# Norms of the keys by one value a token and head, a norm joined to the stage after it, a gate row folded into the experts' sum

## The reference, cut to what matters

```
# first_block, last line
return _rmsnorm(x, final_norm_w)
# second_block
hl = rms_norm(xl, norm1_gain) * (1.0 + sc1l) + sh1l        # 256 latents
hc = rms_norm(xc, norm1_gain) * (1.0 + sc1c) + sh1c        # 256 tokens of ctx
pl = hl @ w_in;  pc = hc @ w_in
# in the rwkv mixer: 512 tokens, 4 heads of 64
kk = hd(k * kk_scale)
kk = kk / jnp.maximum(jnp.sqrt(jnp.sum(kk * kk, axis=-1, keepdims=True)), 1e-12)
# the end
xl = xl + g2l * hierarchical_moe(h2l, *moe_w)
```

## Time and profile before

| | us |
|---|---|
| median of 3 runs | 2254.02 |
| lowest, highest | 2249.06, 2260.88 |
| profiled execution | 2261.8 |
| its span, from the first to the last instruction | 2260.0 |
| TensorE products / weight loads, busy | 2002.8 / 1682.6 |
| VectorE, ScalarE, GpSimd, busy | 1441.5, 1098.9, 146.7 |
| mean granted TensorE clock | 0.928 |

### The profile page before, as it was taken

The page is one execution under the profiler, slowest core; times in us unless marked ns, Lnnn a source line. Parts: engine busy times, 40 slices in busy tenths (PEclk is TensorE's granted clock), DMA queues, the critical chain, the costliest instruction groups (busy, mean ns, idle before and its releaser), DMA issues. The chain is left out here.

```text
span 2260.0 us, 36963 instructions
## 1 busy us (share of the span) xinstructions
PE 2002.8 (89%) x15254; PEld 1682.6 (74%) x15254; DVE 1441.5 (64%) x1794; ACT 1098.9 (49%) x1333; POOL 146.7 (6%) x151
## 2 busy tenths in 40 slices
PE   5788899899788899899959895798899999999997
PEld 5586677899677677799848664686778788788785
DVE  0264345787355444688447938764778788787886
ACT  0353343565254343466346433212567677676674
POOL 0000000000000000000004603620000000000000
PEclk8799799899899889999979987899899999999998
DMA  9764264545266237444342120000689899799896
GB/s 382 275 210 149 94 215 149 192 182 182 104 237 219 100 122 251 157 166 182 130 141 86 55 73 11 14 19 12 229 295 375 300 351 374 272 370 338 303 375 231
DMA packets 153800, 447.54 MB, mean 198 GB/s; under 512 B 10032, under 2 KB 12720, under 8 KB 151088
## 3 DMA queue, kind: packets, MB, share of 16 engines
q1 hardware_dynamic: 153648, 445.41, 54.9%
HBM read 444.33 MB, written 1.05 MB: 197 GB/s over the span
## 5 line engine op out<-in xcount | busy, mean ns | idle before, releaser
L212 DVE TENSOR_TENSOR me_wlow<-me_w,me_whigh 128x2048 fp32r<-128x2048 f32 (+1 forms) x203 | 451.9, 2247 | 107.7 <-ACT me_whigh L207 107.5
L207 ACT ACTIVATE me_whigh<-me_w 128x2048 fp32r<-128x2048 f32 (+1 forms) x203 | 380.2, 1885 | 133.5 <-PE ps L220 124.3
L218 PE MATMUL ps<-me_whigh,me_xhigh 128*128 128x512 f32 x512 | 206.9, 404 | 11.9 <-PEq L119 11.9
L218 PE MATMUL ps<-up_xhigh,ffn_whigh 128*128 128x256 f32 x704 | 201.8, 287 | 8.6 <-DVE ffn_wlow L212 7.0
L220 PE MATMUL ps<-me_whigh,me_xlow 128*128 128x512 f32 x528 | 208.6, 395 | 0.0
L219 PE MATMUL ps<-me_wlow,me_xhigh 128*128 128x512 f32 x512 | 202.0, 394 | 0.0
L219 PE MATMUL ps<-up_xlow,ffn_whigh 128*128 128x256 f32 x704 | 201.0, 286 | 0.0
L220 PE MATMUL ps<-up_xhigh,ffn_wlow 128*128 128x256 f32 x704 | 200.9, 285 | 0.0
L212 DVE TENSOR_TENSOR ffn_wlow<-ffn_w,ffn_whigh 128x2048 fp32r<-128x2048 f32 (+1 forms) x72 | 149.3, 2110 | 60.7 <-ACT ffn_whigh L207 60.6
L212 DVE TENSOR_TENSOR mix_wlow<-mix_w,mix_whigh 128x1024 fp32r<-128x1024 f32 (+2 forms) x116 | 140.4, 1214 | 70.7 <-ACT mix_whigh L207 70.5
L207 ACT ACTIVATE ffn_whigh<-ffn_w 128x2048 fp32r<-128x2048 f32 (+1 forms) x72 | 123.2, 1759 | 47.8 <-PE ps L220 47.8
(11 more groups left out here) (664 smaller groups left out, 4233.6 us busy)
## 6 DMA issues: line engine op xcount, KB each, us to landing
me_w<-w_exp_gate SPq DMA_DIRECT2D x34, 2048.0 KB, 9.6
me_w<-w_exp_up SPq DMA_DIRECT2D x34, 2048.0 KB, 10.2
me_w<-w_exp_down SPq DMA_DIRECT2D x32, 2048.0 KB, 10.2
mix_w<-w_mix SPq DMA_DIRECT2D x108, 512.0 KB, 4.2
mix_aside<-ada_w SPq DMA_DIRECT2D x96, 512.0 KB, 4.6
ffn_w<-ffn_w_up SPq DMA_DIRECT2D x20, 2048.0 KB, 7.6
ada_w<-ada_first SPq DMA_DIRECT2D x12, 2048.0 KB, 23.2
ffn_w<-ffn_w_down SPq DMA_DIRECT2D x8, 2048.0 KB, 7.8
```

The costliest lines, as they stand in the source:

```text
L207: return nc.scalar.activation(high, x, ACT.Copy)
L212: return nc.vector.tensor_tensor(low, x, high.bitcast(F32), ALU.subtract)
L218: nc.tensor.matmul(out, lh, rh, start=start, stop=False)
```

## The change

The last norm of the first block loses its own block and its code moves into `second_projections` (`final_act`, `final_dve`); the transfers are issued there in the order final, vectors, ctx, rows, consts, masks, weights, and each engine waits for the last four small ones at its planned place 13.0 (`arrived`), GpSimd at its start. The norms' planned times go from 1.0 and 2.5 to 4.6 and 7.9, the weights' clock from 17 to 19. The keys' sum of squares is taken with the squares as the stationary operand and `head_pick` (two columns) as the moving one, so that it comes out with tokens on partitions, one value a token and head, 16 a partition; Sqrt, bound and reciprocal work on those, VectorE spreads them over 64 columns each, TensorE transposes the result in eight tiles, and VectorE multiplies `kk` by it out of PSUM. In the experts, g_row is multiplied in when the sum is taken out of PSUM, the additions go straight to x, and each quarter of x is stored as its addition ends.

```diff
-def first_output(core, I, x, coming):
-                for dst, src in coming:
-                    sp.dma_start(dst, src).then_inc(here, 16)
-                sp.wait_ge(here, 16 * len(coming))
...
-        pieces.clock = 17.0
+        pieces.clock = 19.0
...
-                                 (2.5, 1.0)[s], ((0, 1, 2, 3), (4, 5, 6, 4))[s], started) for s in range(2)]
+                                 (7.9, 4.6)[s], ((0, 1, 2, 3), (4, 5, 6, 4))[s], started, (None, final_scaled)[s]) for s in range(2)]
...
+        def final_act(act):
+            yield 0.0
+            for t in range(TT):
+                nc.scalar.activation(hT[1][:, 4 * t:4 * t + 4, :].rearrange("p k n -> p (k n)"), x[:, t, :], ACT.Square,
+                                     accum_out=final_rs[:, t:t + 1]).then_inc(final_squared, 1)
+            yield 2.8
+            act.wait_ge(final_meaned, 1)
+            nc.scalar.activation(final_rs, final_rs, ACT.Sqrt).then_inc(final_rooted, 1)
+
+        def final_dve(dve):
+            yield 2.4
+            dve.wait_ge(final_squared, TT)
+            nc.vector.tensor_scalar(final_rs, final_rs, 1.0 / DM, EPS, ALU.mult, ALU.add).then_inc(final_meaned, 1)
+            yield 3.2
+            dve.wait_ge(final_rooted, 1)
+            nc.vector.reciprocal(final_rs, final_rs).then_inc(final_inverted, 1)
+            dve.wait_ge(final_inverted, 1)
+            dve.wait_ge(final_here, 16)
+            for t in range(TT):
+                nc.vector.scalar_tensor_tensor(out=x[:, t, :], in0=x[:, t, :], scalar=final_rs[:, t:t + 1], in1=final_row,
+                                               op0=ALU.mult, op1=ALU.mult).then_inc(final_scaled, 1)
+
+        def arrived(eng):
+            yield 13.0
+            eng.wait_ge(rest_here, 16 * 4)
+
         def context_act(act):
-            yield 2.4
+            yield 7.8
...
         def setup_dve(dve):
-            yield 0.0
+            yield 2.0
+            dve.wait_ge(vectors_here, 16)
...
+            yield t_low + 12.0
+            pe.wait_ge(kk_own, 4)
+            pe.wait_ge(gate_read, 1)
+            for c in range(NT4):
+                for hp in range(2):
+                    mm = nc.tensor.matmul(low_bank(0)[:, 4 * c + 2 * hp:4 * c + 2 * hp + 2], kn[:, hp, c * P:(c + 1) * P],
+                                          consts["head_pick"], start=True, stop=True)
+            mm.then_inc(kk_summed, 1)
             for hp in range(2):
-                yield t_low + 12.0 + 1.2 * hp
-                pe.wait_ge(kk_own, 4)
+                yield t_keys + 18.0 + 1.2 * hp
+                pe.wait_ge(key_own, spread_made)
                 pe.wait_ge(gate_read, hp + 1)
-                nc.tensor.matmul(low_bank(hp), consts["head_ones"], kn[:, hp], start=True, stop=True).then_inc(kk_summed, 1)
+                for c in range(NT4):
+                    mm = nc.tensor.transpose(low_bank(hp)[:, c * P:(c + 1) * P], kk_spread[:, c, hp], ident)
+                mm.then_inc(kk_summed, 1)
...
             yield t_keys + 16.0
-            dve.wait_ge(kk_rooted, 2)
-            mine(V.tensor_scalar(kn, kn, 1e-12, None, ALU.max))
+            dve.wait_ge(kk_rooted, 1)
+            mine(V.tensor_scalar(kk_rs, kk_rs, 1e-12, None, ALU.max))
             dve.wait_ge(key_own, own)
-            mine(V.reciprocal(kn, kn))
-            yield t_keys + 24.0
+            mine(V.reciprocal(kk_rs, kk_rs))
             dve.wait_ge(key_own, own)
-            mine(V.tensor_tensor(kk, kk, kn, ALU.mult))
+            mine(V.tensor_copy(kk_spread.rearrange("p c h (r n) -> p (c h r) n", r=2), kk_rs.unsqueeze(2).to_broadcast([P, 4 * NT4, HD])))
+            assert own == spread_made
+            for hp in range(2):
+                yield t_keys + 19.2 + 1.2 * hp
+                dve.wait_ge(kk_summed, 2 + hp)
+                mine(V.tensor_tensor(kk[:, hp], kk[:, hp], low_bank(hp), ALU.mult))
...
             @block.sync
             def _(sp):
+                sp.dma_start(final_row, I["final"].to_broadcast([P, DM])).then_inc(final_here, 16)
+                sp.dma_start(*coming["vectors"]).then_inc(vectors_here, 16)
                 sp.dma_start(xc, I["ctx"].rearrange("b (t p) d -> p (b t) d", p=P)).then_inc(ctx_here, 16)
+                for name in ("rows", "consts", "masks0", "masks1"):
+                    sp.dma_start(*coming[name]).then_inc(rest_here, 16)
...
+    def gated_sum(n):
+        cols = slice(512 * n, 512 * (n + 1))
+        return nc.vector.tensor_tensor(yg[:, cols], core.ps[:, 4 + n, :], g_row[:, cols], ALU.mult)
...
-                nc.scalar.activation(yg[:, 0:512], core.ps[:, 4, :], ACT.Copy).then_inc(summed, 1)
...
-                nc.vector.tensor_copy(yg[:, 512:], core.ps[:, 5, :]).then_inc(summed, 1)
+                for n in range(2):
+                    gated_sum(n).then_inc(summed, 1)
...
+            rows = out.rearrange("b (t p) d -> p (b t) d", p=P)
+            for j in range(4):
+                n, t = divmod(j, TT)
+                cols = slice(512 * n, 512 * (n + 1))
+                sp.wait_ge(added, j + 1)
+                sp.dma_start(rows[:, t, cols], x[:, t, cols]).then_inc(stored, 16)
...
-        with core.stage("last_order") as (block, own):
-                for t in range(TT):
-                    order(nc.vector.tensor_tensor(y[:, t, :], y[:, t, :], g_row[:, :], ALU.mult))
-                    order(nc.vector.tensor_tensor(x[:, t, :], x[:, t, :], y[:, t, :], ALU.add))
```

More of the change, by code:

```diff
@@ L859, in kview, with normed_features @@
     return part.rearrange("p (k n) -> p k n", k=kt)
-def normed_features(core, sem, what, x, ident, gain, shift, space, hT, xs, at, banks, ready):
+def normed_features(core, sem, what, x, ident, gain, shift, space, hT, xs, at, banks, ready, made=None):
     nc = core.nc
@@ L2246, with second_projections @@
 SPANS = LEVELS + (P, 2 * P)
-def second_projections(core, I, k, fv, masks, consts, mod, x, X, attended, keys, ycat):
+def second_projections(core, I, k, fv, masks, consts, mod, x, X, attended, keys, ycat, coming):
     nc, ident = core.nc, k["ident"]
@@ L4124, in _, with experts @@
                 V.memset(tile_f[:, TILES:TILES + 1], 0.0).then_inc(consts_set, 1)
-                V.memset(y, 0.0).then_inc(zeroed, 1)
                 V.memset(m["pick_T"][:, :], 0.0).then_inc(zeroed, 1)
-                pool.wait_ge(zeroed, 2)
-def experts(core, k, hT, h_tok, weights, tile_d, tile_i, y, m):
+                pool.wait_ge(zeroed, 1)
+def experts(core, k, hT, h_tok, weights, tile_d, tile_i, x, g_row, out, m):
     nc = core.nc
@@ L4366, in _, with second_block @@
                 add_back(j).then_inc(added, 1)
-def second_block(core, I, k, mod, x, rows):
+def second_block(core, I, k, mod, x, rows, out):
     nc = core.nc
@@ L4404, in second_block @@
         m = expert_space(core, I, mem)
-        second_output(core, I, k, fv, mod, x, ycat, g_row, hT, y, weights, tile_d, tile_i, m)
-        experts(core, k, hT, ycat, weights, tile_d, tile_i, y, m)
-        with core.stage("last_order") as (block, own):
-            @block.vector
-            def _(dve):
-                order = Order(dve, own)
-                for t in range(TT):
-                    order(nc.vector.tensor_tensor(y[:, t, :], y[:, t, :], g_row[:, :], ALU.mult))
-                    order(nc.vector.tensor_tensor(x[:, t, :], x[:, t, :], y[:, t, :], ALU.add))
+        second_output(core, I, k, fv, mod, x, ycat, g_row, hT, weights, tile_d, tile_i, m)
+        experts(core, k, hT, ycat, weights, tile_d, tile_i, x, g_row, out, m)
 def build(nc, I, out):
@@ L4439, in build @@
                                    **{n: rows[:, a:b] for n, (a, b) in R_OFF.items()}), mod_next, x,
-                     (rows[:, :], I["rows"].to_broadcast([P, n_rows])))
-        with core.stage("stored") as (block, stored):
-            @block.sync
-            def _(sp):
-                sp.dma_start(out.rearrange("b (t p) d -> p (b t) d", p=P), x[:, :, :]).then_inc(stored, 16)
-                sp.wait_ge(stored, 16)
+                     (rows[:, :], I["rows"].to_broadcast([P, n_rows])), out)
         core.settle()
```

80 lines of the change are left out of this document (28 added, 52 removed).

## The result

Median 2242.86 us (8 runs, 2222.85 to 2253.16) against 2256.61 us before (8 runs, 2249.06 to 2261.19) beside it: ratio 0.9941, 95% interval 0.9914 to 0.9967, so 13.3 us faster (7 to 19). Measured again later, the unedited changed kernel gave 0.9955 (0.9933 to 0.9977), 10.1 us. The profiled execution took 2241.67 us with a span of 2239.8; its span was 20.2 under that of before. So one question is why it is faster, and another why three measures of one change read 10, 13 and 20.

The account below looks back on a forecast made before the run. TensorE has by far the most busy time, so only its idle stretches and what follows its last product pay. Gains 5.1 + 2.6 + 0 + 7.1 = 14.8 us from the median 2254.02 give 2239.2, range 2232 to 2248.

Parts of the forecast that it names:

- The end, 7.1: Last stage: four operations and two block ends removed, output stored in quarters; 7.1 us gained, bounds 6.3 and 7.6.
- The gate row in each tile, 0: Four expert tiles: gate row multiplied into the sum, covered by TensorE's first two halves; 0, bounds nothing to 0.5 a tile.
- The last norm, 5.1: Norm joined to the projections: TensorE turns 7.6 us earlier, less 2.5 for reordered work; 5.1 gained, bounds 2 to 7.6.
- the walk from there to the first product: Start of projections, both lists walked operation by operation: TensorE turns at 1149.1, first product at 1166.6.
- the queue holds the start: Rival at the projections' start: weights behind seven transfers land at 1156, the joining gives nothing, time 2244.3; chance 0.18.
- Its sign: Projections' start: a wait for sec_w before the first split of x that lasts beyond 1151.
- part 1: The last norm of the first block joined to the projections; 5.1 us gained, bounds 2 to 7.6.
- The keys, 2.6: Keys' norms: shorter reciprocal, but VectorE stands for transposes behind nv's third piece; 2.6 us gained, bounds 1 to 5.
- eight products with two columns replace two of 512: nothing: TensorE ahead of the keys: sixteen narrow products take 1.9 us against 2.0 before, so no gain or loss.
- let the middle shift rigidly: Projections from first product to 1380.9: order unchanged, so the whole stage shifts by the start's 5.1 us.
- slower: the clock: Rival at the first products: thinner work keeps the clock low, 32 us of it takes the whole gain; chance 0.04.

Follow-up runs that it names:

- wide_added: Changed kernel with two unread wide products put back ahead of the sixteen narrow ones; one run, 2245.39 us.
- weights_first: Changed kernel with rows, constants and masks requested behind the first two weights' pieces; ratio to the kernel before 0.9951.
- best: Changed kernel with all edits that gained, plus VectorE's work on the vectors moved behind the scaling of x; 2235.38 us, ratio to the kernel before 0.9918.
- turn_first: Changed kernel with the turning of the keys' reciprocals planned ahead of the third piece of the last projection; ratio to the kernel before 0.9926.

## Why the prediction held, and where it did not

The time on record, 2239.2, lies 3.7 under the first measurement and in the range. Term by term:

- **The end, 7.1.** Measured 7.3 (17.7 to 10.4), within 0.2 in nine of the ten profiles with the edit as it is; in wide_added half clock fell on it, and it was 5.9. The working held down to the last addition. The quarters land 2.0 us after their issue, 2.1 in the working. The Trainium skill (DMA: Bandwidth & Descriptors, section "Anatomy of one DMA — SWDGE (gpsimd) path") gives, by an estimate from its fit, about 2.6 for 256 KB. That section is on transfers that GpSimd issues; these were issued by SyncE, the trace has 2.0, and it decides.
- **The gate row in each tile, 0.** 847.0 before, 847.4 after: held, to within the scatter of that stretch (843.7 to 851.6), and TensorE never stood for a tile's sum.
- **The last norm, 5.1.** The first half held: TensorE turns 7.1 to 8.0 sooner (7.6 on record), and the wait moved to the vectors, as told; what varies is their landing, 3.3 to 4.3 us after their issue in these profiles (4.2 in the changed kernel, 3.5 on record). The step that failed is the walk from there to the first product: 17.5 on record, 19.5 measured, 15.0 before. Of the 2 us, 1.2 lie ahead of the end of ctx's diagonals (7.4 behind the turn instead of 6.2); there the first weights landed at +13.8 instead of +11.8, and with the transfers moved (weights_first) it was 6.2 again. The other 0.8 lies behind them (12.1 to the first product instead of 11.3), in weights_first too; which operation it is stays open. The rival "the queue holds the start" named this mechanism, with weights 5.1 us late that would take the whole gain; they were 2.0 late. Its sign was there: the wait for the first weights lasted, counted from the square and put on the times of the kernel before, to 1152.9 and not to 1151. The term came to 2.8: 29.7, the mean of the seven profiles with part 1 and its lists unedited, against 32.5, the mean of the three without it. That is near the lower bound of 2.
- **The keys, 2.6.** The mechanism was right: the copy done, VectorE stands until TensorE has ended nv's third piece. With the clock up, maximum to the product's end is 5.8 (5.9 in the working) against 8.5, 2.7 gained there, 2.1 at the end of the stage. But TensorE was taken to run at one pace; with the half clock behind the narrow products it is 1.6 us later, and the gain 1.1 there and 0.5 at the stage's end, under the lower bound of 1. The step that failed is "eight products with two columns replace two of 512: nothing". Their own time was right, 1.92; their effect on the clock was not in it.

So the change is worth 2.8 + 0.5 to 2.1 + 7.3, that is 10.6 to 12.2 us, where 14.8 was on record; both measured ratios hold that in their intervals, and the range on record would have held it too. That the first one came close to the term sum is partly the luck of where the clock fell: I had let the middle shift rigidly, and it alone moves between 193 and 200 us with unchanged instructions. The rival "slower: the clock" looked at the first products, and nothing came of it there: nine and eight products at or near half clock. The clock's part in the change was at the other end of the stage.

## What to carry to other kernels

Removing a long operation from one engine pays only if what replaces it on another engine is planned to be ready: here shortening a Reciprocal from 6.55 to 0.26 gave 0.5 us, or 2.1 with the clock up, and moving eight transposes ahead of one piece of a projection gave 3.4 or 1.8 more. When the two sides of a change differ by less than the clock's scatter, compare distances between stations within one trace, and run one unchanged kernel again before explaining a gain. In lists that are merged by planned places, moving one program's places silently reorders everything near it: walk the merged order of each engine, not only of the moved part.

## What the runs showed of the hardware that was not expected

- Sixteen products with two columns in a row, 1.9 us, were followed by 3.3 us at a granted clock of 0.50 in four of eight profiles, with TensorE busy throughout; parted in two groups of eight, or with wide ones ahead, they were not, in one profile each (and in best, parted too). Why four of the eight did not fall is open. It was these narrow products, which replaced wide ones of the same length, that bore on the clock, and not the transposes. The Trainium skill (TensorE: Matmul & The Clock Gate, Part 4), drawn on in the prediction, says that a transpose does not count as busy time for the clock gate in the same way. No run here shows it: behind the eight transposes no fall began in any profile, and in turn_first it had begun ahead of them.
- A copy of 128x1024 out of a broadcast of 16 values took 0.69 us, the price of one plain operand, not 1.22.
- Two TENSOR_SCALAR of 128x512 took 5.00 us together while GpSimd ran its 5.93 of products on the same memory space, and 0.88 when it did not (the rows of the keys above). In the kernel before they shared this with the product ahead of them:

```profile
1380.58 2.99 DVE L2515 TENSOR_TENSOR rw_space<-rw_space 128x1024 f32<-128x1024 f32 x1
1383.61 2.84 DVE L2518 TENSOR_SCALAR rw_space<-rw_space,second_vectors 128x512 f32<-128x512 f32 x2
```

That product took 1.22 in the changed kernel, where it began ahead of GpSimd's. So the three took 5.8 us before and 6.2 after; with GpSimd idle, the same three of the other direction took 2.1.
